# Where the stationary tiles of a matmul lie in SBUF: h, y, m and the value weights moved by 192 and 64 bytes

## The reference, cut to what matters

```python
def swiglu(x, w_in, w_out):
    gu = x @ w_in
    return (jax.nn.silu(gu[..., :D_FF]) * gu[..., D_FF:]) @ w_out        # gated h, then its product
...
    y = from_blocks(hs).astype(u.dtype) * jax.nn.sigmoid(og)             # mLSTM mixer
    return y @ w_out
...
        proj = h @ w_in[l]
        v = proj[..., 2 * A:3 * A].reshape(B, S, N_ATT_HEADS, HEAD_DIM)  # values of a layer
        ...
        mix = jnp.concatenate([att, cnv], axis=-1) @ w_out[l]            # mixes m, then their product
```

## The kernel before, in words

| product | stationary, place | streamed, place | matmuls |
|---|---|---|---|
| feature-wise, 256 tokens | weights, 0 | u, 192 | 2304 |
| feature-wise, 256 tokens, mixer's gates | weights, 0 | u, 64 | 192 |
| feature-wise, 272 tokens | weights, 0 | u or h, 0 | 1984 |
| token-wise on h, y, m | h, y, m, 0 | weights, 0 | 552 |
| token-wise, values | u, 192 | side tiles, 192 | 96 |
| token-wise, gate step | u, 192 | weights, 0 | 48 |

## Time and profile before

### The profile page before, as it was taken

The page is one execution under the profiler, slowest core; times in us unless marked ns, Lnnn a source line. Parts: engine busy times, 40 slices in busy tenths (PEclk is TensorE's granted clock), DMA queues, the critical chain, the costliest instruction groups (busy, mean ns, idle before and its releaser), DMA issues.

```text
span 773.4 us, 14578 instructions
## 1 busy us (share of the span) xinstructions
PE 765.1 (99%) x5754; PEld 722.8 (93%) x5754; DVE 579.8 (75%) x926; ACT 417.2 (54%) x735; POOL 123.1 (16%) x140
## 2 busy tenths in 40 slices
PE   9999999999999999999999999999999999999997
PEld 9999999999999999889999998889999988999985
DVE  6877776699697887588888888677676768567663
ACT  7544444444357576495445443556655457455541
POOL 3800000032230002000000000010054411035510
PEclk9999999999999999999999999999999999999999
DMA  9867666696617564468888786735574571754541
GB/s 349 307 246 248 240 218 232 216 334 208 189 57 259 182 197 145 138 220 309 318 279 310 275 299 214 229 135 190 145 239 137 163 271 44 242 181 135 151 124 54
DMA packets 46402, 162.98 MB, mean 211 GB/s; under 512 B 5200, under 2 KB 6768, under 8 KB 46336
## 3 DMA queue, kind: packets, MB, share of 16 engines
q1 hardware_dynamic: 46336, 162.06, 61.6%
HBM read 160.96 MB, written 1.08 MB: 210 GB/s over the span
## 4 chain that ended last, share of the span: by engine, by line
PE 89%; DVE 5%; ACT 2%; issue 2%; DMA 1%; SPq 0%; POOL 0%; DVEq 0%; POOLq 0%; ACTq 0%
PE ps L374 21%; PE ps L375 20%; PE ps L376 20%; PE ps L824 5%; PE ps L826 5%; PE ps L825 5%; PE ps L766 3%; DVE w L1248 2%; PE ps L681 1%; DVE cv L1553 1%; PE ps L625 1%; PE ps L756 1%; ACT w L875 1%; PE ps L737 1%; PE ps L746 1%
## 5 line engine op out<-in xcount | busy, mean ns | idle before, releaser
L1248 DVE TENSOR_TENSOR w<-raw,w 128x1024 fp32r<-128x1024 f32 x237 | 287.9, 1222 | 124.5 <-ACT w L875 123.9
L374 PE MATMUL ps<-u,w 128*128 128x256 f32 (+1 forms) x1275 | 362.9, 285 | 0.3 <-DVE w L1248 0.3
L376 PE MATMUL ps<-u,w 128*128 128x256 f32 (+1 forms) x1275 | 358.4, 281 | 0.0
L375 PE MATMUL ps<-u,w 128*128 128x256 f32 (+1 forms) x1275 | 358.3, 281 | 0.0
L875 ACT CAST w<-raw 128x1024 fp32r<-128x1024 f32 x237 | 246.1, 1050 | 109.4 <-PE ps L376 77.7
L374 PEld LDWEIGHTS ps<-u,w 128*128 128x128 f32 x1275 | 239.9, 188 | 5.3 <-issue 3.1
L375 PEld LDWEIGHTS ps<-u,w 128*128 128x128 f32 x1275 | 239.9, 188 | 0.1
L376 PEld LDWEIGHTS ps<-u,w 128*128 128x128 f32 x1275 | 239.6, 188 | 0.0
L1948 POOL TENSOR_SCALAR Sb<-Sb,st 128x256 f32<-128x256 f32 x32 | 44.9, 1418 | 94.2 <-DVE st L1717 94.2
L1266 DVE SCALAR_TENSOR_TENSOR acc<-adr,cact,acc 128x1024 f32<-128x1024 f32 x42 | 55.7, 1339 | 0.0
L919 ACT ACTIVATE si<-tmp 128x272 f32<-128x272 f32 (+1 forms) x40 | 17.0, 426 | 65.9 <-DVE tmp L1361 65.9
(11 more groups left out here) (271 smaller groups left out, 982.5 us busy)
## 6 DMA issues: line engine op xcount, KB each, us to landing
raw<-wst SPq DMA_DIRECT2D x245, 512.0 KB, 4.5
adr<-wada SPq DMA_DIRECT2D x48, 512.0 KB, 3.7
Bt<-bias_rows SPq DMA_DIRECT2D x8, 192.0 KB, 3.7
hT<-xT SPq DMA_DIRECT2D x4, 272.0 KB, 4.5
hT<-xtok SPq DMA_DIRECT2D x2, 512.0 KB, 5.8
sq<-nrow SPq DMA_DIRECT2D x2, 512.0 KB, 4.9
g2row<-weight_rows SPq DMA_DIRECT2D x2, 512.0 KB, 6.3
sq<-weight_rows SPq DMA_DIRECT2D x2, 512.0 KB, 5.4
```

The source lines that it names most:

```text
L374: e.matmul(out, a, x1, start=first, stop=False)
L375: e.matmul(out, a, x2, start=False, stop=False)
L376: return e.matmul(out, b, x1, start=False, stop=last)
L1248: e.tensor_tensor(b, r, a.bitcast(F32), ALU.subtract).then_inc(*tick(s_split, k))
```

## The change

Fillers of 192 bytes (48 floats) are put ahead of h1 of the second feed-forward layer, ahead of y1, and ahead of m1 in both layers, so that h, y and m lie at 192 modulo 256, and so does everything that is put behind them in the same stretch: the second modulation's `adr` and `acc`, the mixer's other tiles, the layers' at, cw, cu, st and qk2. The fillers ahead of the side tiles are changed so that these lie at 0. The input u stays at 192 and the weight ring at 0. All 648 token-wise products on h, y, m and of the values then have a stationary operand at 192 and a streamed one at 0, as the gate step has before and after. No instruction is added, removed or moved on any engine, and no queue issues another transfer; only addresses differ.

```diff
--- before.py
+++ after.py
@@ -151,6 +151,8 @@
         ax = None
         for n, row in ((T, TP), (S, S)):
             fx = ExitStack()
+            if n == S:
+                sb("h_shift", [P, 48], F32, fx)
             h1.append(sb(f"h1_{n}", [P, NF, row], F32R, fx)[:, :, 0:n])
             if row % 64:
                 sb(f"gap_{n}", [P, 32], F32, fx)
@@ -162,6 +164,7 @@
             fx.close()
             if ax is None:
                 ax = ExitStack()
+                sb("y_shift", [P, 48], F32, ax)
                 y1 = sb("y1", [P, NH, S], F32R, ax)
                 y2 = sb("y2", [P, NH, S], F32R, ax)
                 zp = sb("zp", [P, 2, T + 3], F32, ax)
@@ -186,7 +189,7 @@
 
         fx = ExitStack()
         sb("over_h1_h2", [P, 2 * NF, S], F32, fx)
-        sb("side0_shift", [P, 48], F32, fx)
+        sb("side0_shift", [P, 64], F32, fx)
         side = [sb("side0", [P, 4, 2, CH], F32R, fx)]
         fx.close()
         qk2 = []
@@ -198,6 +201,7 @@
             sg.append(sb(f"sg{l}", [P, 4, S], F32, lx))
             Sb.append(sb(f"Sb{l}", [P, 4, 2, S], F32, lx))
             PT.append(sb(f"PT{l}", [P, 2, 2, S], F32, lx))
+            sb(f"m_shift{l}", [P, 48], F32, lx)
             m1.append(sb(f"m1{l}", [P, 8, S], F32R, lx))
             m2.append(sb(f"m2{l}", [P, 8, S], F32R, lx))
             at_.append(sb(f"at{l}", [P, 2, S], F32, lx))
@@ -210,13 +214,13 @@
             qk2.append(sb(f"qk2{l}", [P, 8, S], F32R, qx))
             qx.close()
             if l == 0:
-                sb("side1_shift", [P, 48], F32, lx)
+                sb("side1_shift", [P, 16], F32, lx)
                 side.append(sb("side1", [P, 3, 2, CH], F32R, lx))
             lx.close()
             if l == 0:
 
                 sb("over_qk_Vt_sg", [P, 16, S], F32, lx)
-                sb("last_side_shift", [P, 48], F32, lx)
+                sb("last_side_shift", [P, 64], F32, lx)
                 last_side = sb("last_side", [P, 2, CH], F32R, lx)
                 lx.close()
```

## The result

The changed kernel takes 776.68 us (median of 20 runs) against 775.33 for the kernel before (20 runs): ratio 1.0016, 95% interval 1.0010 to 1.0022. That is +1.35 us, inside the predicted range and inside 0.3%; the sum of the prediction said +0.55. The two profiled executions differ by 1.9 us in span, of which 0.8 lies in the first microseconds, ahead of anything that was changed.

A forecast was written before the change was run, and what follows sets the result against it. TensorE's 5754 matmuls, one after the other, were taken to bound the kernel. Terms +1.05 + 0 − 0.5 + 0 = +0.55 us on the profiled 775.25 gave 775.8, plus 0.35 for the median 776.1; range 773.8 to 778.6.

The forecast's parts named there:

- step three: Feature-wise q and k blocks behind the value products, both layers: faster pace taken over, −0.5 us, ends 0 and −0.97.
- Step one: Token-wise products on h and m: 456 matmuls at 2.3 ns more each, +1.05 us.
- settled price: Start-to-start time of a token-wise matmul in an unbroken stream: from 226.7 to 229.0 ns, 2.3 ns more.
- Step two: Value products and products on y, 192 matmuls in short pieces: 0 us, bounds about −0.3 and +0.44.
- The hand-over: Value products at the new distance pass the 113 ns pace to following q and k blocks: 216 × 4.5 ns, −0.97 us.
- Step four: Everything else moved by 192 bytes (casts, splits, qk2 score products, adr loads): 0 us, score products at most ±0.29.
- Rival A: All token-wise products: places don't matter, nothing changes, 775.6 us; chance 0.13.
- Rival B: Long token-wise streams settle at 226.7 ns, feature-wise stretches behind them reach 113: 773.6 us, or 772.3; chance 0.13.
- Rival C: All 648 products lose 4.5 ns each, +2.9 us, or a long feature-wise stretch slows, +4.2: 778.5 or 779.8; chance 0.16.
- long stretch of 939: Feature-wise matmuls after the gate step, now at 113 ns: entered at 118 because y products arrive differently, +4.2 us.

The follow-up runs named there:

- the kernel with distance 128: Against the kernel before, h, y, m at 128 and side tiles at 64, so all 648 token-wise products have operands 128 bytes apart; 780.24 us, ratio 1.0058.
- The kernel at 224: Against the kernel before, h, y, m at 224 and side tiles at 160, putting the value products at distance 32; 781.58 us in a single run.

## Why the prediction was right, point by point

The sign and the size class were right: a little slower, within 0.3%. The main reason was the one given: the gate step in the trace of before was already the changed form. The sum of +0.55 us was too small, against +1.06 in the trace behind the first 21 us and +1.35 between the medians, and the stretches of step three nearly cancelled in a way that was not foreseen.

*Step one* (+1.05 us on h and m): measured +0.56 and +0.37, together +0.93. The settled price came out to a tenth of a nanosecond; m has slower entries already, which the 456 × 2.3 ns did not take off. The run with h alone shows it as a property of those operands.

*Step two* (0 on values and y, ends −0.3 and +0.44): +0.15 and −0.05. The reading of the chain nearly held: 5.55 and 5.56 us where there were 5.52 and 5.50. It was not quite like with like: two filler matmuls stand between the eight transposes and the value products, and none ahead of the gate step's 24.

*Step three* (−0.5, ends 0 and −0.97) is the step that failed: over all feature-wise matmuls of 256 columns +0.07, just outside its upper end. The hand-over was right in layer 1: over the thirteen traces its 192 matmuls are at 117.8 ns in the four kernels that leave its value products at distance 0, at 113.3 in the eight that put them at 192, 64 or 128, and at 117.8 in the one at 32. In the changed kernel that is −0.83 us. It was wrong in layer 0: the first 24 gained nothing, though they did in the run with the side tiles alone. And the prediction put layer 0's other 168 matmuls, behind the transpose, at nothing; they went from 113.3 to 117.8, +0.73. That layer 0's value products bring this about is shown: the 168 are at 117.8 with the side tiles alone, and at 113.3 when side0 stays as before. How it reaches past the transpose is not shown; the run with the transpose moved shows the pace turn there in a kernel whose first block was already fast.

*Step four* (0): casts and splits of the side tiles at 0 take 1053 and 1219 ns against 1045 and 1221, the score products' sum moved by 0.01 us, the adr loads land in 4.0 instead of 3.7 us and nothing waited for it. That difference shows nothing of the place: in the kernels above that leave adr where it was the same row reads from 3.8 to 4.2 us. By the rule of the Trainium skill, page "DMA: Bandwidth & Descriptors", section "How a descriptor splits into AXI transactions", such a row would take one transaction more; no run here measures that.

Rival A, with the rule of the Trainium skill, page "TensorE: Matmul & The Clock Gate", section "Step-by-step: what each phase is for", that the two operands have read ports of their own, fails as a forecast of time: five distances gave settled readings from 226.7 to 233.4 ns on h for one instruction. Where the two operands get in each other's way the runs do not show. Rival B's stretches did speed up in layer 1, but long token-wise streams did not settle at 226.7. Rival C's 4.5 ns would have been too low for the distance of 64 (6.7 ns), had the change been that one; its long stretch of 939 kept 113.3 ns in the changed kernel.

Of the signs that the prediction named, one failed: the first 300 us should have been the same to a few tenths, and were 0.97 us longer, 0.82 of it before 21 us. Its sign of being wrong, an unchanged stretch that carries more than the 648 products, stayed out, but not by much: the products cost +1.03 us together, and the two stretches of step three +0.73 and −0.83.

What stays open is why a distance costs what it costs, when an interruption turns the pace of 256 columns, and why the changed kernel's first block in layer 0 stayed slow where two kernels with the same distance had it fast.

## What to carry to other kernels

Before moving an operand, look in the trace for the same instruction with its operands already at the new distance, and read the price from start times, not from durations or busy shares. Here the long streams paid their settled price, +0.93 us on h and m, and the short pieces hardly any, +0.10 on the values and y. A stretch that was not touched can change its pace because the work ahead of it did, −0.83 and +0.73 us here, so each stretch behind a change needs its own row, those behind an interruption too. Try the sign of a distance too, and each form of matmul by itself: token-wise, 192 and 64 cost 2.3 and 6.7 ns, while feature-wise with 272 columns 64 was the fastest.

## What the runs showed of the hardware that was not expected

The feature-wise stretch of 272 columns has two paces at one and the same places: 125.3 ns in the kernel before, and 126.7 in the profile of the kernel with distance 128, which has its first stages unchanged:

```profile
40.04 0.29 PE L380 MATMUL ps<-u,w 128*128 128x272 f32 x1
...
78.04 0.29 PE L380 MATMUL ps<-u,w 128*128 128x272 f32 x1
```

That is 38.00 us for 300 matmuls instead of 37.60, and 1.3 us over the stretch of 972 there, with granted clocks of 0.998 and 0.999. The kernel at 224, whose first stages are unchanged too, also shows 126.7. What chooses between the two is not known.
